# Hybrid encoder on one core: softmax inverses by DRAM, paired high parts, values a step later, two linear-attention points in one

## What is computed

```python
def attend(blk):                      # latent attention, 4 heads
    s = einsum(qn, k_nope) + einsum(qr, k_rope)
    p = softmax(s * MLA_SCALE)
    return einsum(p, v)

def step(state, inp):                 # gated linear attention, chunks of 64, both directions
    o_inter = einsum(qc * exp(b), state)
    a = einsum(qc, decay, kc)
    o = o_inter + einsum(a, vc)

mixed = concat([o_mla * silu(gate_mla), o_pool * silu(gate_pool), o_gla * silu(gate_gla)])
x + mixed @ w_out                     # then rmsnorm
```

## Time and profile before

| | us |
|---|---|
| median of three executions | 750.37 (746.06 to 754.07) |
| profiled execution, its own time | 750.29 |
| its span, first to last instruction | 748.5 |
| mean granted TensorE clock | 0.987 of full |

### The profile page before, as it was taken

One profiled execution on the slowest core, in us unless ns is written; L12 is line 12 of the kernel. 1 busy time (PEld: TensorE's weight loads), 2 busy tenths in 40 slices (PEclk: granted clock), 3 DMA queues, 4 the chain that ended last, 5 costly groups with the idle time before them and its releaser, 6 DMA issues.

```text
span 748.5 us, 14234 instructions
## 1 busy us (share of the span) xinstructions
PE 721.3 (96%) x5784; PEld 606.4 (81%) x5784; DVE 408.9 (55%) x718; ACT 311.9 (42%) x520; POOL 287.6 (38%) x290
## 2 busy tenths in 40 slices
PE   8999999999999999999999789889989999999996
PEld 6998878878888888888888588788788988888885
DVE  5855877376575543026175757758656654333232
ACT  6554444334423432233223545555554654232321
POOL 3223226366556512122400255553555854322320
PEclk9999999999999999999999889999999999999999
DMA  7613021001122233230235886786886035564441
GB/s 255 183 26 89 28 97 57 30 31 40 63 72 87 73 114 107 92 88 26 63 144 180 249 240 207 230 225 184 264 233 194 1 109 180 176 196 158 139 151 56
DMA packets 65389, 96.14 MB, mean 128 GB/s; under 512 B 6161, under 2 KB 43537, under 8 KB 65330
## 3 DMA queue, kind: packets, MB, share of 16 engines
q1 hardware_dynamic: 53856, 65.34, 30.3%
q10 hardware_dynamic: 11474, 29.96, 10.6%
HBM read 59.30 MB, written 35.00 MB: 126 GB/s over the span
## 4 chain that ended last, share of the span: by engine, by line
PE 76%; DVE 8%; DMA 7%; ACT 4%; POOL 2%; issue 2%; SPq 0%; ACTq 0%; DVEq 0%; POOLq 0%
PE psum L78 20%; PE psum L80 19%; PE psum L79 19%; PE psum L1535 4%; DMA spread_scratch<-a_spread_second 3%; DVE a_top L2082 2%; PE psum L1374 2%; DMA a_turned_lo_third<-spread_scratch 2%; ACT a_weights L1982 2%; POOL a_turned_lo_third L1895 2%; PE psum L1254 1%; DVE g_state L1062 1%; DVE a_weights L2055 1%; DMA a_turned_lo<-spread_scratch 1%; PE psum L1404 1%
## 5 line engine op out<-in xcount | busy, mean ns | idle before, releaser
L78 PE MATMUL psum<-h_hi,z_w_hi 128*128 128x512 f32 x376 | 152.4, 405 | 0.0
L80 PE MATMUL psum<-h_hi,z_w_lo 128*128 128x512 f32 x376 | 146.8, 390 | 0.0
L79 PE MATMUL psum<-h_lo,z_w_hi 128*128 128x512 f32 x376 | 146.6, 390 | 0.0
L78 PEld LDWEIGHTS psum<-h_hi,z_w_hi 128*128 128x128 f32 x376 | 70.6, 188 | 15.9 <-issue 0.7
L80 PEld LDWEIGHTS psum<-h_hi,z_w_lo 128*128 128x128 f32 x376 | 70.6, 188 | 15.4
L79 PEld LDWEIGHTS psum<-h_lo,z_w_hi 128*128 128x128 f32 x376 | 70.7, 188 | 14.0 <-issue 0.7
L1982 ACT ACTIVATE a_weights<-psum,a_bias,mla_q_scale 128x1024 f32<-128x1024 f32 (+1 forms) x48 | 51.0, 1062 | 64.9 <-DVE a_bias L2085 64.9
L805 POOL TENSOR_TENSOR z_w_lo<-z_w_raw,z_w_hi 128x1024 fp32r<-128x1024 f32 x17 | 41.0, 2411 | 94.5 <-ACT z_w_hi L501 92.4
L78 PE MATMUL psum<-o_w_hi,o_m_hi 128*128 128x512 f32 x184 | 72.6, 394 | 0.0
L80 PE MATMUL psum<-o_w_hi,o_m_lo 128*128 128x512 f32 x184 | 72.3, 393 | 0.0
L79 PE MATMUL psum<-o_w_lo,o_m_hi 128*128 128x512 f32 x184 | 72.2, 392 | 0.0
(11 more groups left out here) (281 smaller groups left out, 1656.5 us busy)
## 6 DMA issues: line engine op xcount, KB each, us to landing
z_w_raw<-in_w_z_dram SPq DMA_DIRECT2D x17, 512.0 KB, 3.6
n_x_in<-in_x_dram SPq DMA_DIRECT2D x12, 512.0 KB, 4.3
gates_scratch<-z_gate ACTq DMA_DIRECT2D x24, 256.0 KB, 2.1
spread_scratch<-a_weights ACTq DMA_DIRECT2D x12, 512.0 KB, 5.0
spread_scratch<-a_spread_second ACTq DMA_DIRECT2D x12, 512.0 KB, 6.6
a_turned_lo<-spread_scratch SPq DMA_DIRECT2D x24, 256.0 KB, 5.2
o_x_in<-in_x_dram SPq DMA_DIRECT2D x12, 512.0 KB, 3.6
out_dram<-o_y ACTq DMA_DIRECT2D x11, 512.0 KB, 3.2
```

The lines of the kernel that those rows point to most:

```text
L78: nc.tensor.matmul(out, a_hi, b_hi, start=first, stop=False)
L79: nc.tensor.matmul(out, a_hi, b_lo, start=False, stop=False)
L80: return nc.tensor.matmul(out, a_lo, b_hi, start=False, stop=last)
```

## The change

It does four things. The inverses of the softmax sums go through DRAM: SP stores the two columns of a pair (256 numbers, one by one, `share_dram`) and loads them back spread over all 128 partitions, into the place in `mixed` where the result will stand; `gather` is then one multiplication, and PE's transposes, the copy and `share_row` go. In SP's stream the store stands ahead of the pair's four loads, and waits until the spread inverses of the pair before have landed; the spread load stands behind the four loads and waits until the store has landed. ACT takes both high parts of a pair in step 2p + 5, behind the copy of a latent. `VALUES_AT` moves most pairs one step later. In the linear attention `compare(t)`, `output(t - 1)` and `turn_rows(t - 3)` stand at one point.

```diff
 copy_top:
-                if t >= 2:
-                    act.wait_ge(o_mm, t - 1)
+                if t >= 1:
+                    act.wait_ge(o_mm, t)
 follow (ACT):
                 if at == 0:
+                    if 1 <= t <= TILES:
+                        take_rows(t - 1)
                     if t < TILES:
                         copy_top(t)
+                    if t % 4 == 2 and 6 <= t < TILES + 3:
+                        take_outputs(t // 4 - 1)
...
                 if at == 2:
-                    if t < TILES:
-                        take_rows(t)
-                    if t % 4 == 1 and 1 < t < TILES + 2:
-                        take_outputs(t // 4 - 1)
 DVE, tiles of the front:
-                if t:
-                    scale_rows(t - 1)
-                sum_rows(t)
+                if t >= 2:
+                    scale_rows(t - 2)
+                if t >= 1:
+                    sum_rows(t - 1)
 compare:
-                    pe.wait_ge(o_taken, t)
+                    if t >= 2:
+                        pe.wait_ge(o_taken, t - 1)
 mixing (PE):
-                if p >= 0 and p % 3 == 0 and p // 3 < TILES:
-                    compare(p // 3)
-                if p >= 2 and p % 3 == 2 and p // 3 < TILES + 2:
-                    if p // 3 >= 2:
-                        turn_rows(p // 3 - 2)
-                    if p // 3 < TILES:
-                        output(p // 3)
+                t = p // 3
+                if p >= 0 and p % 3 == 0 and t < TILES + 3:
+                    if t < TILES:
+                        compare(t)
+                    if 1 <= t <= TILES:
+                        output(t - 1)
+                    if t >= 3:
+                        turn_rows(t - 3)
...
-VALUES_AT = tuple(2 * p + 8 for p in range(SPREAD_PAIRS - 2)) + (39, 41, 42, 44, 45, 47, 49, 51)
-LATE_OUTPUTS = SPREAD_PAIRS - 2
+VALUES_AT = (9, 12) + tuple(2 * p + 9 for p in range(2, SPREAD_PAIRS - 3)) + (38, 40, 41, 42, 44, 45, 47, 49, 51)
+LATE_OUTPUTS = SPREAD_PAIRS - 5
...
+            def store_shares(p):
+                if p:
+                    sp.wait_ge(share_passed, 32 * p)
+                sp.wait_ge(share_ready, 2 * p + 2)
+                sp.dma_start(share_dram[p].rearrange("n t -> t n"), share[:, 2 * p:2 * p + 2],
+                             allow_slow_non_contiguous=True).then_inc(share_passed, 16)
+
+            def load_shares(p):
+                sp.wait_ge(share_passed, 32 * p + 16)
+                sp.dma_start(mixed_of(p), share_dram[p].rearrange("n t -> (n t)").partition_broadcast(P))\
+                  .then_inc(share_passed, 16)
 SP, each pair of the first three heads:
+                store_shares(p)
                 for n in range(2):
                     sp.wait_ge(spread_stored[n], 16 * p + 16)
...
+                load_shares(p)
 SP, the last head, behind the output weights:
+            for p in range(SPREAD_PAIRS, PAIRS):
+                store_shares(p)
+                load_shares(p)
 ACT, step m:
-                if 5 <= m < LAST_HEAD + 5:
-                    take_high(m - 5)
                 for p in pair_at(m, VALUES_AT):
                     act.wait_ge(values_done, p + 1)
...
+                if m % 2 and 5 <= m < LAST_HEAD + 5:
+                    take_high(m - 5)
+                    take_high(m - 4)
 gather (DVE):
                 dve.wait_ge(output_done, p + 1)
-                nc.vector.tensor_copy(share_row[:, p % 2, :], psum[:, 6 + p % 2, PAIR:]).then_inc(gathered, 1)
-                dve.wait_ge(gathered, 2 * p + 1)
-                nc.vector.tensor_tensor(keep.mixed[:, h, t:t + PAIR], psum[:, 6 + p % 2, :PAIR],
-                                        share_row[:, p % 2, :], ALU.mult).then_inc(gathered, 1)
+                dve.wait_ge(share_passed, 32 * p + 32)
+                nc.vector.tensor_tensor(mixed_of(p), psum[:, 6 + p % 2, :PAIR], mixed_of(p), ALU.mult).then_inc(gathered, 1)
 output (PE):
-                pe.wait_ge(share_ready, 2 * p + 2)
                 pe.wait_ge(latent_lo_ready, p + 1)
-                for n in range(2):
-                    nc.tensor.transpose(psum[:, 6 + p % 2, PAIR + n * P:PAIR + (n + 1) * P],
-                                        share[:, 2 * p + n:2 * p + n + 1].broadcast_to([P, P]), ident[:, :])
```

More of the change, by code:

```diff
@@ L1217, in split_rope @@
                                             ALU.subtract).then_inc(rope_lo, 1)
+            scale_rows(TILES - 2)
+            sum_rows(TILES - 1)
             scale_rows(TILES - 1)
@@ L1647, in __init__ @@
         self.mix_first = rest("o_mix_first", [P, 4, P])
-        self.share_row = rest("a_share_row", [P, 2, PAIR])
         self.rest = rest
@@ L1771, in portion, with phase_mla_attend @@
     return slice((m % 2) * keys_of(m), (m % 2 + 1) * keys_of(m))
-def phase_mla_attend(nc, cx, block, front, rope_dram, gates_dram, mix_dram, spread_dram, w_out_dram, w_out_loaded, gate_loaded, mix_loaded, psum,
-                     ident, keep):
+def phase_mla_attend(nc, cx, block, front, rope_dram, gates_dram, mix_dram, spread_dram, share_dram, w_out_dram, w_out_loaded, gate_loaded, mix_loaded,
+                     psum, ident, keep):
     with ExitStack() as mem:
@@ L1794, in phase_mla_attend @@
         spread = [weights[:, 2, :], spread_second[:, :]]
-        rest, q_rope, share_row = keep.rest, keep.q_rope, keep.share_row
+        rest, q_rope = keep.rest, keep.q_rope
         top = rest("a_top", [P, STEPS])
@@ L1807, in phase_mla_attend @@
         share_ready = sem("a_share_ready")
+        share_passed = sem("a_share_passed")
         transposed = sem("a_transposed")
@@ L1837, in weights_slot, with mixed_of @@
             return m % 2 if m < LAST_HEAD else (m - LAST_HEAD) % SLOTS
+        def mixed_of(p):
+            return keep.mixed[:, p // (2 * TB), (p % (2 * TB)) * PAIR:(p % (2 * TB) + 1) * PAIR]
         def by_key(parts, p):
@@ L1908, in _ @@
                 if i == 4:
-                    pool.wait_ge(gathered, 3 * TILES + 2)
+                    pool.wait_ge(gathered, SPREAD_PAIRS + 1)
                     multiply(of_heads, heads_gates).then_inc(first_step, 1)
@@ L2091, in _ @@
                     transpose(m - 1)
+                if LAST_HEAD < m <= STEPS:
+                    dve.wait_ge(exp_done, m)
+                if 1 <= m <= STEPS:
                     take_share(m - 1)
@@ L2101, in _ @@
                     tile = m - TURN_LAG
-                    dve.wait_ge(exp_done, tile + 1)
-                    take_share(tile)
                     for n, item in turned_banks(tile):
@@ L2164, in values @@
                 if p >= 2:
-                    pe.wait_ge(gathered, 2 * p - 2)
+                    pe.wait_ge(gathered, p - 1)
                 if p == 0:
@@ L2302, in weight_gates @@
                 nc.gpsimd.tensor_tensor(mix[s][:, :, :], mix[s][:, :, :], gate[s][:, 4:8, :], ALU.mult).then_inc(gated, 1)
-            pool.wait_ge(attend.gathered, 2 * PAIRS)
+            pool.wait_ge(attend.gathered, PAIRS)
             nc.gpsimd.memset(minus_half[:, :], -0.5).then_inc(half_set, 1)
@@ L2484, in hymba_encoder_kernel @@
         spread_dram = {n: scratch(f"spread_scratch{n}", (3, 2, P, n), F32) for n in (BLK, 2 * BLK)}
+        share_dram = scratch("share_scratch", (PAIRS, 2, P), F32)
         z = Region(nc, Z_AT)("z", [P, Z_PLAIN, NT])
@@ L2496, in hymba_encoder_kernel @@
         first_mix_loaded = cx.semaphore("first_mix_loaded")
-        attend = phase_mla_attend(nc, cx, block, front, rope_dram, gates_dram, mix_dram, spread_dram, dram["w_out"], w_out_loaded,
+        attend = phase_mla_attend(nc, cx, block, front, rope_dram, gates_dram, mix_dram, spread_dram, share_dram, dram["w_out"], w_out_loaded,
                                   first_gate_loaded, first_mix_loaded, psum, ident, keep)
```

1 line of the change is left out of this document (removed).

## The result

The changed kernel took 935.88 us, the median of 4 runs (934.03 to 941.03), against 750.17 (746.06 to 754.07) for the kernel before beside it: a ratio of 1.2487, with a 95% interval of 1.2403 to 1.2572. It is slower by 186 us where 739 us, 1.5% faster, had been forecast, and far outside the range of 722 to 756.

The account below looks back on a forecast made before the run. PE's work plus its gaps was taken as the bound, gaps and low clock making 23.2 us. Merged points 3.5, inverses' transposes 3.8 and later values 4.4 sum to 11.7 us: 750.3 becomes about 739 us, range 722 to 756.

Parts of the forecast that it names:

- The store of 4-byte pieces: SP's store of a pair's inverses to DRAM, 256 pieces of 4 bytes: between nothing and 0.9 us more DMA.
- The spread load: SP's load of the inverses to all partitions, 128 pieces of 1 KB over 16 engines: 0.46 us.
- Rival (c): SP's serial stream sets the pace: 12 heavy pairs each 1.0 us over budget, plus low clock, 766 us; chance 0.15 with (d).
- the last part: List of signs to look for; for serial loads, SP waiting for spread inverses and load issues over 10 us apart.
- Its low clock: In rival (c), all nine waits of PE bring the low clock: five more stretches at 1.7 us, 8.5 us.
- (d): `gather` waits for the inverses; nearly excluded, some seven steps of 2 us or more between; chance 0.15 together with (c).
- Merged points: Linear attention, 11 tiles with one point in place of two: less change-over on PE, 2.8 to 4.0 us, taken as 3.5.
- The inverses' transposes: PE's transposes ahead of `output` go, 0.22 us a pair: 3.8 us saved, between 2.0 and 5.8.
- The values a step later: Latent attention: one more `scores` before PE asks for values; shorter waits and less low clock, 4.4 us, from -9 to 23.2.
- net for a wait: PE's wait for POOL: 2.1 us gained less later loads and more DMA, -1.0 to +1.6, middle +0.3 us.

Follow-up runs that it names:

- rows: Changed kernel with DVE turning each pair's inverses first, so that two stores carry four pieces of 128 bytes each, SP's waits unchanged: 758.24 us, ratio 1.0136.
- the spread load a pair later: Changed kernel with stores of 128-byte rows and also the spread load issued a pair behind, on its own semaphore: 743.81 us, 0.9936 of the kernel before.

## Why the prediction was wrong, point by point

- **The store of 4-byte pieces: the step that failed.** It stood at 0 to 0.9 us, "near the lower end". It takes 8.0 us with nothing beside it and 9.3 in the attention. Three things went wrong in that step. The upper bound was the time of 256 pieces in the DMA engines, at the queue's average of 57 ns a piece; the time lies elsewhere, as the same 256 pieces land in 1.6 us at 64 bytes apart, and side by side, in the last head, their packets are through 1.1 us behind the issue while the store lands at 8.0. The row that drew the value down was a constant of 0.5 KB that landed in 2.1 us; that is a load, whose pieces go to 128 partitions, and says nothing of small pieces written side by side into DRAM. And with no row near, the bound should have been left open, not closed by an average; as it was, no chance was left for anything above 770 us.
- **The rule that was weighed against it.** The Trainium skill, on the page "DMA: Bandwidth & Descriptors", has in "Rules for kernel authors" that a strided last dimension makes one descriptor per element, and in "Specifications" that pieces under 512 bytes are read, modified and written back. That spoke against the store, and the runs bear out the direction: 8.0 us. The figure that I drew from it, 0.9 us, was too small by a factor of 9; that was my own pricing by the average piece. The measurement decides: at 64 bytes apart the same small pieces cost next to nothing, so smallness alone isn't the price.
- **The spread load** was put at 0.46 us too, its time in the DMA engines, and that was counted twice, in SP's stream and as more DMA. It lands in 5.7 us (median), and SP waits 101.0 us for it. With a cheap store that costs far less than the loss: in the run with the pieces 64 bytes apart SP still waits 76.7 us for such a load, and the kernel is 6 us slower than before.
- **What the store holds up had no term at all.** I counted its time on engines that are 79% busy, not that other transfers land later meanwhile: 83 us.
- **Rival (c), the serial stream.** Place and sign were right: SP waits 22 times for the spread load of the pair before, and load issues stand 16.4 us apart, as the last part said they would if this rival came true. Its price, 1.0 us a heavy pair, was off because the store's was. With a cheap store the serial stream costs 14.4 us (rows, 758.24, against the spread load a pair later, 743.81), near the 12 us that (c) had ahead of the low clock. Its low clock came, too, with 34.5 us in place of 8.5.
- **(d), `gather` waiting for the inverses, "nearly excluded".** In the first three heads it did not decide. In the last head it did: 50.2 us in the window above, 59.8 with the wait ahead of it. The step 2p + 12 holds for the first pairs; in the last head `VALUES_AT` and `LATE_OUTPUTS` put `gather` at step 2p + 7 or 2p + 8. There a pair needs 13 us of store and load in a row, more than its steps of PE take, and the pairs queue up.
- **Merged points: right.** 3.5 us forecast, 4.0 measured (2.4 to 5.8), and 2.5 to 2.7 seen directly at the first `scores`. One sign came out the other way: `choose` was to have less idle time ahead, and has 1.9 us a tile more. The working itself had it start later behind ACT, so that sign was misread from it.
- **The inverses' transposes: mechanism right, size too high.** `output`'s first product takes the 0.12 us forecast. Of the 3.8 us, nothing that can be told arrives without the lag, and some 2.4 with it (ratios 0.9968 and 0.9936, whose intervals touch), the low end of 2.0 to 5.8.
- **The values a step later: wrong.** 4.4 us forecast, none measured (the run with lag and paired high parts alone, 749.16 us). That the lag hides POOL's low parts was right, with 16.1 us going to 1.9. The step that failed is "net for a wait": it took PE's wait for POOL as the only limit and didn't ask what ends next. It was the bank freed by `gather`, the next exponential and the latent's low part. The working itself said that a saving ahead of a wait only makes the wait longer, and didn't apply it here.

## What to carry to other kernels

A transfer's price isn't its bytes, nor its pieces by an average: ask where the pieces land, and when no row of the trace shows a store of that shape, leave its upper bound open and let it weigh in the chances. Before a result goes through DRAM, lay it in rows on the chip (one turn on DVE took the loss from 186 to 10 us here) or keep the pieces 64 bytes apart (no run here reads them back from there), and issue the read a pair later than the write. When a lag hides one wait, list what the engine needs next before counting the gain.

## What the runs showed of the hardware that was not expected

- 256 pieces of 4 bytes, written side by side, land in 8.0 us; 64 bytes apart in 1.6. 128 of them side by side take 7.6, nearly as long as 256, so the number does not set the time; it looks as if pieces that share one short stretch of DRAM follow one another, and different stretches go on beside each other. How long a stretch is was not measured, as no distance between side by side and 64 bytes was tried. Were it 64 bytes, its 16 pieces would take (8.0 - 1.6) / 15 = 0.43 us each, an estimate from these two rows. With pieces of 8 bytes side by side it is 2.7 to 4.1 us, less than that picture gives; why stays open.
- Such a store holds up other transfers while it is under way: a load of 256 KB issued 0.4 us behind it landed in 12.1 us in place of 2.7, and 18 stores that nobody awaited cost 83 us. ACT's stores, on another queue, slowed down with them (4.0 us before, 10.5 beside the unawaited stores, for 256 KB).
- One row of 1 KB read to 128 partitions took 2.9 to 3.2 us alone, 128 rows of 1 KB 2.0; in the changed kernel's last head, right behind the store of that row, 4.9, and about 3 there where the load read another row (the run with the pieces 64 bytes apart).
